# Second block of a two-block transformer kernel: the rotations beside attention are laid on other steps, the fourth row tile of a group is copied one step later, and the last turn moves among the gates

## The reference, cut to what matters

```python
aq = apply_rope_2(rms_norm(aq.reshape(B, S, A_HEADS, HEAD_DIM), a_q_norm), cos, sin)
ak = apply_rope_2(rms_norm(ak.reshape(B, S, A_HEADS, HEAD_DIM), a_k_norm), cos, sin)
...
ya = sparse_attention(aq, ak, av, iq, ik, iw, k_sel).reshape(B, S, D_A)
...
yb = diff_attention(bq, bk, bv, lam)
```

## Time and profile before

| | us |
|---|---|
| median of 3 runs (lowest, highest) | 2322.22 (2318.85, 2324.87) |
| the profiled execution | 2324.22 |
| its span in the trace | 2322.7 |
| PE busy, share of the span | 2211.7, 95% |
| DVE, ACT, POOL busy | 1240.6, 844.0, 354.7 |
| the changed stretch, first layer (y = 12 to 53) | about 857 to 947 us of the span |
| the changed stretch, second layer | about 1644 to 1734 us |

### The profile page before, as it was taken

One profiled execution on the slowest core, in us unless ns is written; L12 is line 12 of the kernel. 1 busy time (PEld: TensorE's weight loads), 2 busy tenths in 40 slices (PEclk: granted clock), 3 DMA queues, 4 the chain that ended last, 5 costly groups with the idle time before them and its releaser, 6 DMA issues.

```text
span 2322.7 us, 28099 instructions
## 1 busy us (share of the span) xinstructions
PE 2211.7 (95%) x10765; PEld 1676.8 (72%) x10765; DVE 1240.6 (53%) x2363; ACT 844.0 (36%) x1486; POOL 354.7 (15%) x273
## 2 busy tenths in 40 slices
PE   7999988879888999999999999999999999999999
PEld 4885676643336776778878888887677787888887
DVE  4743446641226877665654334459766755443442
ACT  4434442421113446443432222344554434332221
POOL 0111023000001554331000000035433200000000
PEclk9999899979999999999999999999999999999999
DMA  8217210299995222221323333232222123323322
GB/s 308 56 55 244 92 37 11 106 379 409 409 409 210 70 82 63 73 73 42 104 91 100 99 92 100 84 94 77 69 64 75 62 65 99 100 91 100 100 82 81
DMA packets 175581, 288.01 MB, mean 124 GB/s; under 512 B 13487, under 2 KB 125657, under 8 KB 175449
## 3 DMA queue, kind: packets, MB, share of 16 engines
q1 hardware_dynamic: 173152, 278.73, 35.7%
q0 software_dynamic: 1152, 4.19, 0.5%
q10 hardware_dynamic: 1144, 3.29, 0.4%
HBM read 281.98 MB, written 4.19 MB: 123 GB/s over the span
## 4 chain that ended last, share of the span: by engine, by line
PE 79%; DVE 10%; DMA 4%; ACT 4%; issue 2%; SPq 1%; POOL 0%; DVEq 0%; ACTq 0%
PE PS L677 21%; PE PS L679 20%; PE PS L678 20%; PE PS L1452 3%; PE PS L2445 3%; PE PS L2484 2%; PE PS L1434 2%; PE PS L2504 1%; PE PS L1444 1%; PE PS L1620 1%; DMA ONCE<-in_w_gate_dram 1%; DMA AR<-in_w_mod_dram 1%; DVE AL L859 1%; SPq L3639 1%; PE PS L1631 1%
## 5 line engine op out<-in xcount | busy, mean ns | idle before, releaser
L677 PE MATMUL PS<-OPH,WHI 128*128 128x512 f32 x1224 | 499.0, 408 | 12.3 <-DVE OPL L1491 6.1
L679 PE MATMUL PS<-OPH,WLO 128*128 128x512 f32 x1224 | 482.5, 394 | 0.0
L678 PE MATMUL PS<-OPL,WHI 128*128 128x512 f32 x1224 | 481.2, 393 | 0.0
L628 ACT ACTIVATE WHI<-RAW 128x1024 fp32r<-128x1024 f32 (+2 forms) x282 | 292.8, 1041 | 457.7 <-PE PS L679 449.2
L649 DVE TENSOR_TENSOR WLO<-RAW,WHI 128x1024 fp32r<-128x1024 f32 (+1 forms) x187 | 224.2, 1201 | 373.8 <-ACT WHI L628 373.8
L665 POOL TENSOR_TENSOR WLO<-RAW,WHI 128x1024 fp32r<-128x1024 f32 (+1 forms) x95 | 229.7, 2420 | 945.5 <-ACT WHI L628 939.4
L677 PEld LDWEIGHTS PS<-OPH,WHI 128*128 128x128 f32 x1224 | 232.3, 190 | 78.0 <-issue 24.6
L679 PEld LDWEIGHTS PS<-OPH,WLO 128*128 128x128 f32 x1224 | 232.1, 190 | 50.5
L678 PEld LDWEIGHTS PS<-OPL,WHI 128*128 128x128 f32 x1224 | 232.8, 190 | 43.6 <-issue 1.0
L677 PE MATMUL PS<-WHI,OPH 128*128 128x512 f32 (+2 forms) x568 | 228.8, 403 | 6.4 <-DVE OPL L2145 2.4
L679 PE MATMUL PS<-WHI,OPL 128*128 128x512 f32 (+2 forms) x568 | 216.6, 381 | 0.0
(11 more groups left out here) (446 smaller groups left out, 3237.0 us busy)
## 6 DMA issues: line engine op xcount, KB each, us to landing
RAW<-in_w_in_dram SPq DMA_DIRECT2D x102, 512.0 KB, 3.7
RAW<-in_w_ffn_in_dram SPq DMA_DIRECT2D x88, 512.0 KB, 3.5
RAW<-in_w_ffn_out_dram SPq DMA_DIRECT2D x40, 512.0 KB, 3.5
RAW<-in_w_mod_dram SPq DMA_DIRECT2D x36, 512.0 KB, 4.7
ONCE<-in_w_down_dram SPq DMA_DIRECT2D x35, 512.0 KB, 15.7
RX<-in_w_gate_dram SPq DMA_DIRECT2D x33, 512.0 KB, 15.7
RAW<-in_w_out_dram SPq DMA_DIRECT2D x24, 512.0 KB, 4.4
ONCE<-in_w_up_dram SPq DMA_DIRECT2D x20, 512.0 KB, 14.7
```

The costliest lines, as they stand in the source:

```text
L628: hi.up(A.e.activation(q.fhi, q.flat, ACT.Copy), ("w", q.i))
L677: T.e.matmul(o, a[0], b[0], start=first, stop=False)
L678: T.e.matmul(o, a[0], b[1], start=False, stop=False)
L679: return T.e.matmul(o, a[1], b[0], start=False, stop=last)
```

## The change

The two helpers that place the rotations beside attention, `each_third` for the stages and `rows_due` for the row copies, are partly replaced. Nothing is added to the work or taken from it: no operation changes its size, and the queues of POOL, SP and the DMAs keep their order.

```diff
         def rows_due(y, lag):
             j = y - 12 - lag
-            return (j // 16, j % 16) if 0 <= j < 48 and j % 16 < 4 else None
+            if 0 <= j < 48 and j % 16 < 3:
+                return j // 16, j % 16
+            return (j // 16, 3) if 0 <= j < 48 and j % 16 == 4 else None
...
         def turn_due(y):
-            return each_third(y, 9)
+            return {21: (0, 0), 24: (0, 1), 30: (0, 2), 33: (0, 3), 37: (1, 0), 40: (1, 1), 46: (1, 2), 53: (1, 3)}.get(y)
+
+        def rope_part(y, lags):
+            for a in range(2):
+                for t in range(4):
+                    if lags[t] and y == 12 + 16 * a + 3 * t + lags[t]:
+                        return a, t
...
+                        if (g, n, j) == (0, 1, 0):
+                            pe_rope_turns(first + 8)
...
                 act_half_between(l, y)
-                at = each_third(y, 3)
-                if at and at[1] % 2:
-                    act_rope_root(first + 4 * at[0] + at[1] - 1, 2)
-                at = each_third(y, 2)
+                at = rope_part(y, (2, 2, 2, 2))
                 if at:
                     act_rope_squares(first + 4 * at[0] + at[1])
+                at = rope_part(y, (None, 2, None, 3))
+                if at:
+                    act_rope_root(first + 4 * at[0] + at[1] - 1, 2)
                 at = rows_due(y, 1)
...
-                at = each_third(y, 7)
+                at = rope_part(y, (7, 7, 9, 9))
                 if at:
                     dve_rope_end(first + 4 * at[0] + at[1])
-                at = each_third(y, 2)
+                at = rope_part(y, (2, 2, 3, 3))
                 if at:
                     dve_rope(first + 4 * at[0] + at[1])
```

## The result

The changed kernel takes 2331.35 us, the median of 9 runs (2326.32 to 2336.83); the kernel before took 2324.87 us in 9 runs on the same chip (2317.9 to 2326.95). The ratio is 1.0039 (95% interval 1.0028 to 1.0049): slower by 9.1 us (6.5 to 11.4). That is over the 7.0 us which the prediction named as what a measurement can tell, though the interval's lower end lies just under it. The profiled execution took 2326.32 us with a span of 2324.6 us and is the quickest of the nine; the second profile taken of this kernel took 2329.65 us.

A forecast was written before the change was run, and what follows sets the result against it. PE, busy 95% of the span, bounds the kernel, so only its waits count. Terms of +1.5 us a layer (+3.0 for two) plus +4.4 for the clock give +7.4 on the median of 2322.22: 2329.5 us, range 2318 to 2334.

The forecast's parts named there:

- the forecast case: In each layer a bank wait of about 4.5 us at y = 35, then a clock fall; 2328 to 2331.5 us, chance 0.50.
- bank wait at y = 35: Step 11, behind unit 7's values: PE waits for ACT's late fourth row copy of `ak`, +4.5 us a layer.
- The clock: Behind the wait at y = 35, PE's granted clock falls to 0.50 in each layer: 2.2 us each, +4.4 us.
- rival of a clock that holds: The wait at y = 35 comes, but the clock keeps its level in one or both layers; 2325 to 2327.5 us, chance 0.20.
- Wait (a): Step 7, after the first `aq` turn: PE's 1.84 us wait for DVE's least goes, -1.84 us a layer.
- Wait (b): Step 8, second `aq` turn: PE's wait of 1.64 us becomes some 0.8, -0.85 us a layer.
- Cover at y = 19: Root one part earlier on ACT: the row copy still ends 0.4 us before PE wants the bank, so no wait.
- wait (c): Step 16, y = 48: PE's 1.30 us wait for DVE's copy of `av`'s first tile keeps its chain, 0.
- later turns: Turns of `aq` 2 and 3, `ak` 2 and 3: the same number of transposes in other gaps, 0.
- short waits: Two short waits for the least behind later turns may go, -0.3 us a layer.
- no bank wait: Rival: the copy of `ak`'s fourth row tile makes no wait; 2315.2 to 2316.8 us, chance 0.18.
- more waits: Rival: a second wait of 1 to 2 us in each layer, +10 to +13, 2332 to 2335 us, chance 0.12.

The follow-up runs named there:

- E2: Changed kernel with 18 extra unused 128x512 matmuls on PE ahead of y = 35, filling the wait; 2326.17 us, ratio 1.0022 to the kernel before.
- E4: Kernel before with only the fourth row copy of each group one part later; 2331.13 us, ratio 1.0036.
- E1: Changed kernel with the row copy put ahead of squares and root in ACT's part; 2324.58 us, ratio 1.0015 to the kernel before.
- E3: Kernel before with only the sums and cosines of `aq`'s tiles 3 and 4 later on DVE; 2318.32 us, ratio 0.9984.
- E6: Kernel before with later sums and cosines of `aq`'s tiles 3 and 4, and DVE copying `av`'s first row tile at y = 44; 2314.79 us, ratio 0.9965.
- E9: Changed kernel with 9 extra unused 128x512 matmuls ahead of y = 35, half filling the wait; 2328.93 us, ratio 1.0037 to the kernel before.

## Why the prediction was right

It said 2329.5 us, and the median is 2331.35; the forecast case came, a bank wait in each layer with a fall of the clock behind it. The mechanism is right. That the sum comes out so close is in part luck. It had +1.5 us a layer without the clock and 2.2 for the clock, 3.7 together. The traces show +2.2 without the clock (E2), and for the clock 1.5 in the profile, so two errors of 0.7 cancel there; in the mean of both profiles the clock's part is 2.0. Step by step:

- **The bank wait at y = 35**: right, with place, releaser and chain. From the start of unit 7's values to the end of the row copy are 4.79 us (898.31 to 903.10), where 4.78 had been worked out (906.56 to 911.34), and PE goes on 0.05 us later. The 4.23 us in the row count from the end of the values' group, 0.61 behind its start; counted as the prediction did, from where the next matmul would start, 0.36 behind it, the delay is 903.15 - 898.67 = 4.48 us, against 4.5. E4 shows that the late row copy makes 2.86 of it, and the rest is the root moved ahead of it.
- **The clock**: right that it falls, in both layers and both profiles. The term was 2.2 us a layer, and measured 1.50 to 2.61, 1.97 in the mean of four (E2 as the base). The rival of a clock that holds did not come at 4.2 us of waiting in four stretches, nor at 2.61 us in two (E4). The prediction said of this rival that it is decided by the length of the wait; at 2.09 us the clock fell in one layer and held in the other (E1), so the length alone does not decide.
- **Wait (a)**: -2.03 us against -1.84; the start-to-start count takes in a little more than the row's idle time.
- **Wait (b)**: 0.60 us against 0.8. The rotation ends 5.4 us behind unit 3's values (870.88 to 876.29), 5.5 had been worked out. The pair L856 and L859 ahead of it took 1.41 us (873.48 to 874.89), 1.4 had been taken. But the sum is off. I looked at the second turn only, and not at what L859 of the fourth tile, moved behind unit 8's least, has queued behind it on DVE: the turned tile's copy L917. With it the scores of unit 9 lose 1.2 us. So (b) is no gain of 0.85 us but a loss of 0.26: in E3 directly, and in the changed kernel as -0.91 + 1.17. This is the term that was mis-sized. With (a) it makes 1.77 us a layer in E3, where 2.7 had been worked out.
- **Cover at y = 19, wait (c), later turns, short waits**: right, at 0 and -0.3 (from unit 12's scores to unit 13's are 7.18 us before and 6.88 in E2). The row copy ahead of y = 19 ended at 863.09 and PE came to it at 863.55, so the cover was 0.46 us where 0.4 had been worked out. At y = 48 PE waits 1.30 us as before. E6 shows that (c) is what was said, a wait for the copy of `av`'s tile on DVE and not for L628, which the earlier trace rows names.
- **The rivals**: "no bank wait" is out; so is "more waits", by the list, unless one calls the 1.2 us at unit 9 that. Its +10 us lies within the interval of the time all the same. The +7.5 of the two profiled stretches and the +9.1 (6.5 to 11.4) of the medians do not contradict each other; the longer clock falls of the second profile would give 1.7 us more.
- **PE's time is the kernel's time**: the prediction said that all that follows runs behind PE without a wait. The list has waits between the two layers, 4.0 us before and 4.1 after; they hardly moved, so the sum does not suffer.

The Trainium skill's rule on table loads ("ScalarE: Activation LUTs", "What ACT_TABLE_LOAD costs") would have made the delay an estimated 5.9 us by its 1380 ns of drain; the trace has 4.48 us, with the root 0.01 us behind the load. The Trainium skill's rule that the clock is halved when TensorE idles ("TensorE: Matmul & The Clock Gate", "Part 1: The HAM clock gate") agrees with the rows at 4.23 and 2.61 us; at 1.84 and 2.15 us of waiting the clock kept its level in the profiles, and at 2.09 us in one layer of two.

## What to carry to other kernels

Before a copy that empties a bank is moved later by one part, read who wants that bank next and which instructions stand ahead of the copy in its new part; here the loss was a chain that started at PE's own instruction, and its length could be read off the old trace to 0.1 us, in three kernels (4.5 and 4.48, 2.9 and 2.86, 2.3 and 2.34). Then follow what is queued behind a moved instruction to the next copy that frees a bank, and not only to the next wait that you know. Price a stop of PE of some us with a fall of its clock behind it (here another 1.5 to 2.6 us on 4.2). Measure a moved stretch from the start of one instruction to that of another, as a wait inside a group of matmuls is in no list of waits.

## What had not been expected

- **DVE beside POOL.** L859, the same 128x512 product, takes 0.69 us at 874.20 and 1.87 us at 879.12. POOL had begun a product of its own just before the second:

```profile
878.05 2.39 POOL L665 TENSOR_TENSOR WLO<-RAW,WHI 128x1024 fp32r<-128x1024 f32 x1 [0.18 <-ACT WHI L628]
...
935.76 2.82 DVE L880 TENSOR_TENSOR AL<-AL,CO 128x512 f32<-128x512 f32 x1
```

  L859 ends at 880.99, 0.55 us behind POOL's end. The other rows of these stretches show the same order. L880, of 0.69 us by itself, is begun here 0.12 us behind POOL's next L665 (935.64, 2.39 us long), takes 2.82 us and ends at 938.58, again 0.55 us behind POOL's end. L859 in the kernel before does so at 876.02 (1.23 us, 0.54 behind the end of the L665 that began at 873.98). Where DVE's product begins first, it keeps its 0.69 us (L859 at 918.26, POOL at 918.47), and the sum L856, which has one input, takes 0.67 us in the midst of POOL's product (878.41). So what a product costs on DVE depends on whether POOL's is already running, and the change put L859 of the fourth tile just behind one. The Trainium skill, page "GPSIMD Engine Reference", section "1. Specifications", says that GpSimd shares its SBUF interfaces with VectorE and contends with instructions that have two SBUF inputs; L859 and L880 are such. The rows agree. No run moved POOL's product alone.
- **Stops of PE, and the clock behind them.** A wait of 1.84 us had no fall behind it; at 2.09 us the clock fell in one layer and not in the other (E1), at 2.15 us it did not (E9's profile), at 2.61 us it fell in both (E4). The same wait of 4.23 us had falls of different length in two executions (1.5 and 2.6 us lost).
